# Reading matmul operands as two interleaved halves instead of backwards, with interleaved sums in PSUM

## What is computed

```python
def swiglu(h, wg, wu, wd):
    return (jax.nn.silu(h @ wg) * (h @ wu)) @ wd       # 1024 -> 2816 -> 1024

# for each of the two layers
x = x + 0.5 * swiglu(rmsnorm(x, ...), ffn1_w_gate, ffn1_w_up, ffn1_w_down)
h = rmsnorm(x, norm_mix)
y = even_mixer(h, ...)     # layer 0: h @ w_in (1024 x 4104), two recurrences, o @ w_out (1024 x 1024)
y = pool_mixer(h, ...)     # layer 1: u = h @ w_in (1024 x 1024), trailing means, a small product per group
x = x + y
x = x + 0.5 * swiglu(rmsnorm(x, ...), ffn2_w_gate, ffn2_w_up, ffn2_w_down)
# at the end a last rmsnorm, and all recurrent states are returned
```

## Time and profile before

| what | value |
|---|---|
| median of 3 runs | 996.99 us |
| the profiled execution's own time | 997.9 us |
| its span in the profile | 996.2 us |
| granted TensorE clock over the span | 0.999 of full |
| PE busy | 986.7 us (99%) |
| DVE busy | 661.2 us (66%) |
| ACT busy | 511.6 us (51%) |
| DMA traffic | 178.03 MB, mean 179 GB/s |

### The profile page before, as it was taken

One profiled execution on the slowest core, in us unless ns is written; L12 is line 12 of the kernel. 1 busy time (PEld: TensorE's weight loads), 2 busy tenths in 40 slices (PEclk: granted clock), 3 DMA queues, 4 the chain that ended last, 5 costly groups with the idle time before them and its releaser, 6 DMA issues.

```text
span 996.2 us, 21003 instructions
## 1 busy us (share of the span) xinstructions
PE 986.7 (99%) x8294; PEld 975.0 (98%) x8294; DVE 661.2 (66%) x895; ACT 511.6 (51%) x717; POOL 115.3 (12%) x185
## 2 busy tenths in 40 slices
PE   9999999999999999999999999999999999999998
PEld 9999999999998899999999999999999999999998
DVE  6865665589887887766654486666546986666443
ACT  6544443576785846544443474444336364444334
POOL 5800000010022402000000020005001020000001
PEclk9999999999999999999999999999999999999999
DMA  8565566555453535655555556556554545555551
GB/s 280 195 207 184 175 217 218 185 179 167 146 169 108 151 127 170 195 195 184 186 181 183 184 170 210 189 187 211 189 181 139 173 150 189 180 195 186 182 186 45
DMA packets 49837, 178.03 MB, mean 179 GB/s; under 512 B 5952, under 2 KB 5968, under 8 KB 49760
## 3 DMA queue, kind: packets, MB, share of 16 engines
q1 hardware_dynamic: 46368, 165.50, 50.9%
q0 software_dynamic: 3120, 11.35, 3.9%
q10 hardware_dynamic: 288, 0.32, 0.1%
HBM read 171.19 MB, written 6.52 MB: 178 GB/s over the span
## 4 chain that ended last, share of the span: by engine, by line
PE 94%; DVE 4%; issue 1%; ACT 1%; DVEq 0%; ACTq 0%
PE ps L1877 29%; PE ps L1879 29%; PE ps L1878 29%; DVE w_lo L1315 1%; DVE PT L1283 1%; PE ps L1665 1%; PE ps L2035 1%; PE ps L1701 0%; PE ps L1717 0%; PE ps L1932 0%; PE ps L1937 0%; PE ps L1940 0%; ACT xw_hi L652 0%; DVE xw_lo L1336 0%; DVE PT L1262 0%
## 5 line engine op out<-in xcount | busy, mean ns | idle before, releaser
L642 ACT CAST w_hi<-raw 128x1024 fp32r<-128x1024 f32 x308 | 320.5, 1047 | 398.8 <-PE ps L1879 394.3
L1315 DVE TENSOR_TENSOR w_lo<-raw,w_hi 128x1024 fp32r<-128x1024 f32 x308 | 374.4, 1231 | 181.4 <-ACT w_hi L642 178.4
L1877 PE MATMUL ps<-xw_hi,w_hi 128*128 128x264 f32 x1440 | 408.6, 284 | 0.3 <-DVE w_lo L1315 0.3
L1878 PE MATMUL ps<-xw_lo,w_hi 128*128 128x264 f32 x1440 | 407.5, 283 | 0.0
L1879 PE MATMUL ps<-xw_hi,w_lo 128*128 128x264 f32 x1440 | 407.5, 283 | 0.0
L1877 PEld LDWEIGHTS ps<-xw_hi,w_hi 128*128 128x128 f32 x1440 | 270.7, 188 | 1.1 <-DVE w_lo L1315 0.7
L1878 PEld LDWEIGHTS ps<-xw_lo,w_hi 128*128 128x128 f32 x1440 | 270.7, 188 | 0.1
L1879 PEld LDWEIGHTS ps<-xw_hi,w_lo 128*128 128x128 f32 x1440 | 270.7, 188 | 0.0
L1877 PE MATMUL ps<-a_hi,w_hi 128*128 128x264 f32 x704 | 199.2, 283 | 0.0
L1878 PE MATMUL ps<-a_lo,w_hi 128*128 128x264 f32 x704 | 199.2, 283 | 0.0
L1879 PE MATMUL ps<-a_hi,w_lo 128*128 128x264 f32 x704 | 199.2, 283 | 0.0
(11 more groups left out here) (379 smaller groups left out, 791.4 us busy)
## 6 DMA issues: line engine op xcount, KB each, us to landing
raw<-in_ffn_w_down SPq DMA_DIRECT2D x88, 512.0 KB, 3.8
raw<-in_ffn_w_gate SPq DMA_DIRECT2D x87, 512.0 KB, 4.2
raw<-in_ffn_w_up SPq DMA_DIRECT2D x87, 512.0 KB, 4.2
raw<-in_w_in_even SPq DMA_DIRECT2D x32, 512.0 KB, 3.9
raw<-in_w_out_even SPq DMA_DIRECT2D x8, 512.0 KB, 3.7
raw<-in_pool_w_in SPq DMA_DIRECT2D x8, 512.0 KB, 3.4
out<-SBUFS POOLq DMA_DIRECT2D x4, 512.0 KB, 4.1
x<-in_x SPq DMA_DIRECT2D x4, 264.0 KB, 5.2
```

The lines of the kernel that those rows point to most:

```text
L642: nc.scalar.copy(w_hi[:, w % SPL, :], raw[:, w % RAW, :]).then_inc(hi_done, 1)
L1315: nc.vector.tensor_tensor(w_lo[:, w % SPL, :], raw[:, w % RAW, :], w_hi[:, w % SPL, :].bitcast(F32), ALU.subtract).then_inc(lo_done, 1)
L1877: mm(out, wh, hi, start=first, stop=False)
L1878: mm(out, wh, lo, start=False, stop=False)
```

## The change

The moving operand is no longer read backwards but by turns from its two halves: column 0, column 132, column 1, column 133, and so on (`in_turns`). The output is written in natural order. So the sum of token t lies in PSUM column 2t for t < 132, and in column 2(t-132)+1 for the others. Every DVE instruction that reads such a sum reads the bank with a step of two columns, first the even, then the odd ones (`apart`, `apart2`), and gives its other operands and its output as two halves (`halved`, `halves2`). The two turned blocks of the input projection take four pieces instead of three. Matmuls that are not part of the threefold products stay as they are, as does the number of matmuls.

```diff
+        def in_turns(a):
+            return a.rearrange("p (two n) -> p n two", two=2)
+        def halved(a):
+            return a.rearrange("p (two n) -> p two n", two=2)
+        def apart(a):
+            return a.rearrange("p (n two) -> p two n", two=2)
+        def apart2(a):
+            return a.rearrange("p a (n two) -> p a two n", two=2)
+        def halves2(a):
+            return a.rearrange("p a (two n) -> p a two n", two=2)
...
+        turned_by_halves = [(slice(0, P), slice(0, P)),
+                            (slice(2 * P - 1, 2 * P - 1 - (HALF - P), -1), slice(P, HALF)),
+                            (slice(2 * P - 1 - (HALF - P), P - 1, -1), slice(HALF, PROMPT)),
+                            (slice(PROMPT, TOK), slice(PROMPT, TOK))]
...
-                for to, tok in turned if b in (4, 5) else [(slice(0, TOK), slice(0, TOK))]:
-                    ins = V.tensor_tensor(PT[:, 2 * b:2 * b + 2, to], ps[:, z:z + 2, tok], rstd2[:, :, tok], ALU.mult)
+                if b in (4, 5):
+                    for to, tok in turned_by_halves:
+                        at = slice(2 * (tok.start % HALF) + tok.start // HALF,
+                                   2 * (tok.start % HALF) + tok.start // HALF + 2 * (tok.stop - tok.start) - 1, 2)
+                        ins = V.tensor_tensor(PT[:, 2 * b:2 * b + 2, to], ps[:, z:z + 2, at], rstd2[:, :, tok], ALU.mult)
+                else:
+                    ins = V.tensor_tensor(halves2(PT[:, 2 * b:2 * b + 2, :]), apart2(ps[:, z:z + 2, 0:TOK]), halves2(rstd2),
+                                          ALU.mult)
...
-                V.tensor_tensor(up[:, pair, PAD:], ps[:, z:z + 2, 0:TOK], rstd2, ALU.mult).then_inc(st("pool_u"), 1)
+                V.tensor_tensor(halves2(up[:, pair, PAD:]), apart2(ps[:, z:z + 2, 0:TOK]), halves2(rstd2), ALU.mult)\
+                    .then_inc(st("pool_u"), 1)
...
-                    nc.vector.scalar_tensor_tensor(x[:, d, :], ps[:, (z + 2) % 8 if n == 5 else d, 0:TOK], sc, x[:, d, :], ALU.mult, ALU.add)\
+                    nc.vector.scalar_tensor_tensor(x[:, d, :] if n == 5 else halved(x[:, d, :]),
+                                                   ps[:, (z + 2) % 8, 0:TOK] if n == 5 else apart(ps[:, d, 0:TOK]), sc,
+                                                   x[:, d, :] if n == 5 else halved(x[:, d, :]), ALU.mult, ALU.add)\
...
-                    nc.vector.tensor_tensor(pr[:, :, :], ps[:, st4:st4 + 2, 0:TOK], rstd2, ALU.mult)\
+                    nc.vector.tensor_tensor(halves2(pr[:, :, :]), apart2(ps[:, st4:st4 + 2, 0:TOK]), halves2(rstd2), ALU.mult)\
...
-                    nc.vector.tensor_tensor(pr[:, :, :], sg[:, :, :], ps[:, st4:st4 + 2, 0:TOK], ALU.mult)\
+                    nc.vector.tensor_tensor(halves2(pr[:, :, :]), halves2(sg[:, :, :]), apart2(ps[:, st4:st4 + 2, 0:TOK]), ALU.mult)\
...
-                out, hi, lo = out[:, ::-1], hi[:, ::-1], lo[:, ::-1]
+                hi, lo = in_turns(hi), in_turns(lo)
                 mm(out, wh, hi, start=first, stop=False)
...
-                    outs = [ps[:, bank + j, 0:TOK][:, ::-1] for j in range(2)]
+                    outs = [ps[:, bank + j, 0:TOK] for j in range(2)]
...
-                            mm(outs[j], w_hi[:, s, cols(y, j)], xw_hi[:, k, ::-1], start=k == 0, stop=False)
+                            mm(outs[j], w_hi[:, s, cols(y, j)], in_turns(xw_hi[:, k, :]), start=k == 0, stop=False)
```

More of the change, by code:

```diff
@@ L1936, in pieces @@
                         for j in range(2):
-                            mm(outs[j], w_hi[:, s, cols(y, j)], xw_lo[:, k, ::-1], start=False, stop=False)
+                            mm(outs[j], w_hi[:, s, cols(y, j)], in_turns(xw_lo[:, k, :]), start=False, stop=False)
                         pe.wait_ge(*formed(lo_done, "lo_part", s, y))
                         for j in range(2):
-                            ins = mm(outs[j], w_lo[:, s, cols(y, j)], xw_hi[:, k, ::-1], start=False, stop=k == KD - 1)
+                            ins = mm(outs[j], w_lo[:, s, cols(y, j)], in_turns(xw_hi[:, k, :]), start=False, stop=k == KD - 1)
                     return ins
```

## The result

| | before | after |
|---|---|---|
| median of 4 runs | 997.04 us | 946.18 us (945.99 to 946.92) |
| ratio after/before | | 0.949, 95% interval 0.947 to 0.951 |
| the profiled execution's own time | 997.9 us | 945.99 us |
| its span | 996.2 us | 944.3 us |

The kernel is faster by 51 us. The page of the kernel after: span, busy time and the chain that ended last, to be held against the earlier trace rows.

The account below looks back on a forecast made before the run. PE was taken as the bound: 7392 threefold matmuls 120 ns apart, 887 of 996 us. Terms -56.8 + 1 + 1 + 0.5 = -54.3 us gave 943.6 from 997.9, stated as 943 us; range 938 to 1027.

Parts of the forecast that it names:

- the 8 ns: Threefold products on PE: the 120 ns between matmul starts exceeds the 112 ns floor by 8 ns.
- Two blocks from different places, used by turns, overlap in their fetching: Threefold products' moving operand: comes in blocks of four columns, and two open blocks overlap, so 112 ns.
- Not from the direction: fp32r operand reads: natural and backward order cost about the same, 0.438 against 0.447 ns per column.
- Step 1: Threefold products outside the pooling stretch: operand by turns saves 8 ns on each of 7104 matmuls, -56.8 us.
- Step 2: What is late next: new waits on DVE, +1 us at three FFN-end places and +1 us in the input projection.
- Step 3: DVE readers with step two in PSUM: 5% slower, mostly hidden, +0.5 us at the ends of FFNs and output projection.
- Step 4: Two more pieces of `evac` and two more views: below 0.2 us each beside PE, counted as nothing.
- every column fetches anew: Rival for the threefold products: 222 ns between starts and 1751 us, or 472 ns and +3,600 us; chance 0.18.

Follow-up runs that it names:

- p3: Kernel after, but the operand read by turns from two neighbouring blocks of four columns (0, 4, 1, 5, 2, 6, 3, 7, ...): 946.50 us.
- p4: Kernel after, but the operand read by turns in pairs (0, 1, 132, 133, 2, 3, 134, 135, ...): 1374.45 us.
- p10: Kernel after, but reading 0, 2, 1, 3, 2, 4, 3, 5, ..., covering only columns 0 to 133: 951.72 us.
- e1_natural: Kernel before, but operands and output of the threefold products in natural order: 1003.38 us against 997.60, ratio 1.005.
- e3_readers_only: Kernel after, but with the backward matmuls of the kernel before, keeping the new step-two readers: 997.57 us, ratio 1.000 to the kernel before.
- p1: Kernel after, but the operand read with step two, all even columns and then all odd ones: 1867.59 us.
- p2: Kernel after, but the operand read with step four (0, 4, 8, ..., 260, then 1, 5, ...): 1893.30 us.
- p8: Kernel after, but the order changed only within each block of four columns (0, 2, 1, 3, then 4, 6, 5, 7, ...): 1002.66 us.

## Why the prediction was right, and what was off

The forecast was 943 us, the result 946.18. Against the profiled execution, 943.6 was forecast and 945.99 measured: 2.4 us too low.

- **What bounds the kernel, and the 8 ns.** Right. The distance of 120 ns was the handle, and 112 the floor from the two fp32 rows. All of the gain is that distance.
- **"Two blocks from different places, used by turns, overlap in their fetching".** I took this reading because it was the one in which the change gains, and no row spoke for it; that it gave the right number is in part luck. It holds for the kernel after and p3, but not as a rule. Had the change been p4, two blocks by turns in pairs, the same reading would have forecast 112 ns, and the kernel ran at 171. What the runs show in its place is that the even and the odd places of the order must each use all four columns of a block before they go on; the blocks need not lie in different halves (p3), and may be partly the same (p10).
- **"Not from the direction".** Right for the gain (`e1_natural` gains nothing), not exact: 1 ns of difference. The reading of the earlier trace rows could not show it: it went through the shortest of 16 records and the tail of another kind of matmul, and it took the 2 ns off one side only. Taken off both, it is 222/512 = 0.434 against 0.447 ns per column, natural order faster by 3%, where the run has it slower by 1%.
- **Step 1, -8 ns.** The step that was mis-sized. In the second FFN of layer 0 the lead grows from 18.32 to 30.14 us over 1576 matmuls, which is 7.5 ns each: 7104 x 7.5 = 53.3 us instead of 56.8. The starts in the earlier trace rows have two decimals and cannot tell 7.5 from 8; what gave 8 was the floor of 112, where 112.5 was measured (2.5 ns over the 110, not 2). The matmul count was right: the 308 slots named for the kernel before leave out the four of the opening, 312 in all, and 308 x 24 = 7392. That nothing would be won in the pooling stretch was right: 36 us for the same 261 matmuls.
- **Step 2, +2.** Right in size, not in place. What gaps between threefold products have over the usual distance adds up to 3.0 us before and 6.0 after; 0.7 of the difference lies in the pooling stretch, and the other +2.3 is what the step was about. At the three places that I named, the eighth `x_lo` or `xw_lo` before an FFN's last sums, PE has a gap of 217 ns each (191.0, 549.8, 729.3 us), 0.1 us more than the distance, and one of 152 to 154 ns right before it, so together 0.4 of the +1 that I gave them. The input projection has +0.2 of its +1. The larger ones I had not named: 0.55 us for `w_lo` at 34.3 us, behind the opening, and 0.60 us for `xw_lo` at the end of the output projection (368.2). Outside the stream of threefold products two more waits grew, by 0.3 us (269.2, the recurrences' `DEC`) and 0.5 us (550.9, `w_lo` behind a norm), and some smaller ones, 0.5 us near 22.5 us and 0.3 us at 936.2 us the largest of them.
- **Step 3, +0.5.** It was 0 within the noise: the ratio of `e3_readers_only` is 1.000. I took the price of an SBUF row with step 2, a single instruction against a group of six. Its 5% does not show in PSUM.
- **Step 4, 0.** Right: DVE's busy time is 661.1 against 661.2 us.

The sum with measured sizes: -53.3 + 2.3 + 0.3 + 0.5 = -50.2. The opening, which I had left out, gives -1.5 more (the lead at 15.3 us of the kernel before). That is -51.7, of 51.9 measured. It closes more tightly than the working deserves: the smaller waits are not in it (+0.8 for the two named), and the distance over the whole trace, 7.6 ns shorter and not 7.5, makes up for them (-0.7).

**The rival "every column fetches anew".** Its chance of 0.18 was not foolish. Its lower price, 222 ns, is near the 237 and 240 ns of p1 and p2, and p1 differs from the change by no more than the order of the letters in one pattern. The runs fit blocks of four columns: p3, in blocks of four, has 112.5 ns, and p8, the same pattern in pairs, 121. The Trainium skill, "Advanced Engine Details and Errata", section "Memory Cachelines", gives SBUF lines of 16 bytes, four fp32 columns; with that these runs agree. It also says that a different line with each access is penalised, and there the measurement decides against it: in the changed kernel each column lies in another line than the one before, and it shares the shortest distance of all, 112.5 ns, with p3. If the rule is read for every second column, it fits p1 and p2; but two columns per line still leave 120 ns against the 112.5 of four.

## What to carry to other kernels

Hold the distance between starts of a matmul stream against its columns at the granted clock plus 2.5 ns, and take it from the count in a long window. If it is above, the moving operand may be short of supply, and fp32r operands are best given so that the even and the odd places of the reading order each walk through neighbouring columns, as two interleaved halves do. All this was measured at 264 columns. The reordering of the sums can then be left to the vector readers, which took a step of two columns in PSUM at no cost; but an order that looks much alike can double the time, so try each on the chip.

## What was not expected of the hardware

- Twelve orders for 264 reads of fp32r columns took from 112.5 to 240 ns, with the granted clock at 1.00 in all (eleven read each column once; p10 reads 134 of them, most of them twice).
- Natural order of operands and sums is slower than backward order: 121.1 against 120.1 ns per matmul over the trace, and 1.005 times the kernel's time.
- 264 columns at 112.5 ns are 2.5 ns over the 110 ns of the full clock, with a weight load of 128x128 in each.
- The last matmuls of `x_hi`, which took 3 ns more than the others when read backwards (119 to 127 ns, mean 123, in the earlier trace rows), took no more when read by turns. Over the whole trace the products of `x_hi` took 120.8 ns backwards where the others took 120.0, and by turns 112.5 like the others.
